# A hybrid DeltaNet and sliding-window trunk in fp32 on one core: decay chain, first chunk, norms by halves, and the order around the attention

## The chip, the cores and the metric

One core of one Trainium2 chip runs the whole program in one launch. The metric is device time in microseconds, from launch to the end of the last instruction, the median of three runs of the kernel before.

## What is computed

One sequence of 256 tokens of width 1024 goes through two layers, with an RMS norm ahead of each part:

```
h = x
h = h + gated_deltanet(norm(h))      # proj 1024 -> 4096 + 16, conv of 4 taps, silu, 8 heads of 128
h = h + swiglu(norm(h))              # dense, inner width 2816
k, v = norm(h) @ w_kv                # 4 kv heads of 64
h = h + attention(norm(h), k, v)     # 16 query heads, window 128, sinks, relative bias
h = h + moe(norm(h))                 # top 2 of 8 experts, inner width 3584
out = norm(h)

norm(x) = x * rsqrt(mean(x * x) + 1e-6) * w

# the delta rule, per head, over 4 chunks of 64 tokens, state S = 0 at first
v_new = u - w @ S
o     = q_dec @ S + attn @ v_new
S     = S * exp(g_last) + k_dec.T @ v_new
# g = cumsum(-exp(a_log) * softplus(a + dt_bias)), beta = sigmoid(b)
```

All inputs and the output are fp32.

## The kernel before

The program is written engine by engine: each of the five engines has its own block, a list of instructions in a fixed order, and semaphores (names `s_...`, `m_...`, `f_...`) tie them together. No scheduler sets an order; what a line waits for stands ahead of it as `wait_ge`. The tokens are two tiles of 128 (`NT`), a 1024-wide row of a tile is one row of SBUF. Products in the dense parts are made in three passes, high by high, low by high and high by low (`L1478` to `L1480` for TensorE); ScalarE rounds weights to their high part (`w_round`, L750), VectorE forms the rest (`w_rest`, L1144). The stages, in TensorE's order:

- **Projection and convolution.** 24 tiles of 128 columns of q, k and v come out of TensorE in six groups ("chunks" of weights) of four. Per tile ScalarE scales the first tap out of PSUM (`first_tap`, L663), VectorE adds the others (`convolve`, L974) and ScalarE applies silu (`conv_silu`, L649); at the first tile of a group `first_tap` also rounds a half of the next group's weights before and after the silu (`q_round`, L644). The decay chain (L676 to L681 on ScalarE: exponentials of the b columns, of `a_log` and of the a columns, then a logarithm, and a few small operations on VectorE between) stands behind the eighth tap. `squared` (L685) squares all of q, later all of k; `L1547` on TensorE sums the squares by matmuls with one column.
- **The delta rule.** TensorE computes u and w in four groups (L1631, L1641), ScalarE and VectorE evict them. Then the scan over four chunks (`n`): eight products w with S (L1654), eight q with S (L1660), VectorE's subtraction, eight products for the new state (L1667), eight with the masked scores (L1674). S is set to zero by a memset on GpSimd ahead of it.
- **Output projection.** Per tile, `turn_out` (L1682) transposes the output in two halves of four, ScalarE and VectorE evict one half each (`s_ot`), `project` (L1690) multiplies by two weight halves, and VectorE adds to h (`add_h`, L1135).
- **A norm** (`k` from 0 to 5: ahead of the DeltaNet, the dense SwiGLU, k and v, the attention, the router, and at the end) is a chain: ScalarE squares and sums a tile of 1024 columns (`squares`, L605), GpSimd makes the reciprocal root (`norm_rstd`, L510 and L511), VectorE multiplies by it and by the weights (`norm_x`, L933), TensorE transposes (`turn`, L1452), and ScalarE and VectorE evict to high and low parts (`turned`, L614 or L620, and L943 or L1155).
- **Dense SwiGLU**: eleven slices of the inner width, then keys and values.
- **Attention** in four groups of heads (`g`): VectorE and ScalarE prepare the queries (`queries`, L831), TensorE the scores, ScalarE the exponentials (`exps`, L841), TensorE transposes the weights and multiplies with v (`values`, L1849), VectorE divides (L1278), and `merge` (L1880) is the output product, by tiles of 128 columns of heads.
- **Router and experts**: 8 passes over 7 slices each, with weights of 2 MB that come by DMA, and then the last norm and the two transfers of the output at the end of the block of SyncE.

```
for n in range(8):                       # ScalarE, before
    first_tap(n)
act.wait_ge(s_tail, 1)
act.activation(beta, tail[:, :, 0:8], ACT.Exp, scale=-1.0).then_inc(s_bexp, 1)
```

## Time and profile before

| | |
|---|---|
| median of three runs | 1562.39 us (1561.8, 1562.39, 1566.46) |
| the profiled execution | 1561.36 us, of which the span 1559.5 |
| busy TensorE, its weight loads | 97%, 80% |
| busy VectorE, ScalarE, GpSimd | 72%, 58%, 7% |
| DMA | 438 MB, 281 GB/s on the mean |

Times of the trace are microseconds from the start of the span, and each number of the profile belongs to the one profiled execution. A row of a timeline is start, length, engine, line of the program, operation, output and inputs with their shapes, how many, and in square brackets how long the engine stood idle before it and what ended that. A row of waits is the waiting operation, what it waited for, and in microseconds the sum, how many, and the longest. A row of windows is given with its columns. The names in it are buffers: `ws` the large work space, `sm` the small one, `bank` the PSUM, `xn` the normed tokens, `cst` the constants.

### The profile page before, as it was taken

What the parts mean: (1) busy time and instruction counts of PE and PEld (TensorE: products, weight loads), DVE (VectorE), ACT (ScalarE), POOL (GpSimd) and SP (SyncE); (2) the same over time, 40 slices, a digit from 0 to 9 for tenths busy, and PEclk for the clock granted to TensorE, in tenths of its full rate; (3) what the DMA queues carried; (4) which work ended last, traced back from release to release, by engine and by line L of the source; (5) the groups of instructions that cost most, each with busy time, mean ns of one, the idle gap of its engine ahead of it and who ended that gap; (6) DMA issues with size and microseconds to landing.
All of it is one profiled execution on the core that took longest, in us unless ns stands there. A gap on an engine that the chain in (4) does not pass through costs nothing.

```text
span 1559.5 us, 22166 instructions
## 1 busy us (share of the span) xinstructions
PE 1505.5 (97%) x8759; PEld 1255.0 (80%) x8759; DVE 1126.2 (72%) x1048; ACT 903.2 (58%) x841; POOL 102.4 (7%) x63
## 2 busy tenths in 40 slices
PE   7999998999999889999999999999999999999996
PEld 6895976999987557888888888888888888888885
DVE  4656254555432348998998998889898889889885
ACT  4641133344422335776777777777777777677773
POOL 2331010000000000000000000000000000000000
PEclk9999999999999989999999999999999999999999
DMA  7432104655463156999999999999999999999992
GB/s 266 151 133 81 37 21 133 214 186 188 134 243 135 55 189 240 394 393 365 388 395 354 384 383 375 392 386 346 392 393 364 393 375 362 370 395 381 379 383 85
DMA packets 194028, 438.01 MB, mean 281 GB/s; under 512 B 5216, under 2 KB 28032, under 8 KB 193856
## 3 DMA queue, kind: packets, MB, share of 16 engines
q1 hardware_dynamic: 188944, 423.64, 73.9%
q0 software_dynamic: 2736, 9.31, 2.4%
q10 hardware_dynamic: 2304, 4.43, 0.8%
q8 instruction: 33, 0.54, 0.2%
q14 instruction: 11, 0.09, 0.0%
HBM read 429.48 MB, written 7.88 MB: 280 GB/s over the span
## 4 chain that ended last, share of the span: by engine, by line
PE 91%; DVE 4%; ACT 3%; issue 1%; DMA 1%; POOL 0%; DVEq 0%; ACTq 0%; POOLq 0%
PE bank L1478 24%; PE bank L1480 24%; PE bank L1479 24%; PE bank L1821 2%; PE bank L1690 2%; PE bank L1880 2%; PE bank L1513 2%; PE bank L1988 2%; PE bank L1866 1%; DVE ws L974 1%; DVE weights_lo L1144 1%; PE bank L1452 1%; PE bank L1620 1%; PE bank L1603 1%; PE bank L1547 1%
## 5 line engine op out<-in xcount | busy, mean ns | idle before, releaser
L1144 DVE TENSOR_TENSOR weights_lo<-weights,weights_hi 128x2048 fp32r<-128x2048 f32 (+1 forms) x396 | 823.5, 2122 | 152.3 <-ACT weights_hi L750 150.8
L750 ACT ACTIVATE weights_hi<-weights 128x2048 fp32r<-128x2048 f32 (+1 forms) x396 | 687.3, 1786 | 250.7 <-DMA weights<-in_moe_w_up 87.3
L1478 PE MATMUL bank<-weights_hi,expert_x_hi 128*128 128x512 f32 x896 | 354.9, 396 | 1.4 <-DVE expert_x_lo L1357 1.1
L1480 PE MATMUL bank<-weights_hi,expert_x_lo 128*128 128x512 f32 x896 | 349.4, 390 | 0.0
L1479 PE MATMUL bank<-weights_lo,expert_x_hi 128*128 128x512 f32 x896 | 349.2, 390 | 0.0
L1478 PE MATMUL bank<-weights_hi,hidden_hi 128*128 128x512 f32 x528 | 207.3, 393 | 2.1 <-DVE hidden_lo L1182 2.1
L1479 PE MATMUL bank<-weights_lo,hidden_hi 128*128 128x512 f32 x528 | 205.6, 389 | 0.0
L1480 PE MATMUL bank<-weights_hi,hidden_lo 128*128 128x512 f32 x528 | 205.6, 389 | 0.0
L1480 PEld LDWEIGHTS bank<-weights_hi,expert_x_lo 128*128 128x128 f32 x896 | 168.2, 188 | 36.4
L1478 PEld LDWEIGHTS bank<-weights_hi,expert_x_hi 128*128 128x128 f32 x896 | 168.3, 188 | 35.4 <-DVE expert_x_lo L1357 1.2
L1479 PEld LDWEIGHTS bank<-weights_lo,expert_x_hi 128*128 128x128 f32 x896 | 168.4, 188 | 33.4
L1478 PEld LDWEIGHTS bank<-weights_hi,hidden_hi 128*128 128x128 f32 x528 | 99.2, 188 | 22.5 <-issue 1.7
L1480 PEld LDWEIGHTS bank<-weights_hi,hidden_lo 128*128 128x128 f32 x528 | 99.1, 188 | 20.9
L1479 PEld LDWEIGHTS bank<-weights_lo,hidden_hi 128*128 128x128 f32 x528 | 99.2, 188 | 19.8
L1478 PE MATMUL bank<-x_hi,weights_hi 128*128 128x256 f32 x320 | 91.0, 284 | 1.2 <-issue 1.2
L1480 PE MATMUL bank<-x_hi,weights_lo 128*128 128x256 f32 x320 | 90.6, 283 | 0.0
L1479 PE MATMUL bank<-x_lo,weights_hi 128*128 128x256 f32 x320 | 90.5, 283 | 0.0
L767 ACT ACTIVATE ws<-bank 128x512 f32<-128x512 f32 x67 | 39.7, 593 | 84.9 <-PE bank L1480 84.7
L1478 PEld LDWEIGHTS bank<-x_hi,weights_hi 128*128 128x128 f32 x320 | 61.4, 192 | 1.8 <-issue 1.4
L1479 PEld LDWEIGHTS bank<-x_lo,weights_hi 128*128 128x128 f32 x320 | 61.4, 192 | 0.4
L1480 PEld LDWEIGHTS bank<-x_hi,weights_lo 128*128 128x128 f32 x320 | 61.4, 192 | 0.0
L1478 PE MATMUL bank<-qkv_x_hi,qkv_hi 128*128 128x256 f32 x192 | 57.5, 300 | 3.2 <-DVE ws L974 3.2
(306 smaller groups left out, 1553.3 us busy)
## 6 DMA issues: line engine op xcount, KB each, us to landing
weights<-in_moe_w_down SPq DMA_DIRECT2D x56, 2048.0 KB, 9.5
weights<-in_moe_w_up SPq DMA_DIRECT2D x56, 2048.0 KB, 9.5
weights<-in_moe_w_gate SPq DMA_DIRECT2D x55, 2048.0 KB
weights<-in_a_w_in SPq DMA_DIRECT2D x8, 2048.0 KB, 9.0
weights<-in_ffn_w_up SPq DMA_DIRECT2D x11, 1024.0 KB, 5.3
weights<-in_ffn_w_gate SPq DMA_DIRECT2D x11, 1024.0 KB, 7.9
weights<-in_ffn_w_down SPq DMA_DIRECT2D x11, 1024.0 KB, 4.9
weights<-in_a_w_out SPq DMA_DIRECT2D x2, 2048.0 KB, 7.9
```

What stands on the lines that cost most here:

```text
L750: act.activation(hi[:, j * n:(j + 1) * n], slot[k][:, j * n:(j + 1) * n], ACT.Copy).then_inc(w_hi[k], 1)
L767: act.activation(act_h, bank[0][:, :], ACT.Silu).then_inc(m.act, 1)
L974: i_ = dve.scalar_tensor_tensor(out=dst[:, sh:T], in0=src[:, 0:T - sh], scalar=cw[:, w:w + 1], in1=dst[:, sh:T], op0=ALU.mult, op1=ALU.add)
L1144: dve.tensor_tensor(to[:, c], slot[k][:, c], hi[:, c].bitcast(F32), ALU.subtract).then_inc(w_lo[k], 1)
L1478: pe.matmul(dst, ah, bh, start=start, stop=False, skip_group_check=True)
L1479: pe.matmul(dst, ah, bl, start=False, stop=False, skip_group_check=True)
L1480: return pe.matmul(dst, al, bh, start=False, stop=stop, skip_group_check=True)
L1513: m = pe.matmul(b[:, :], xt[:, kt, t * P:(t + 1) * P], g8[c % 3][:, kt, :], start=kt == 0, stop=kt == KT - 1)
L1690: m = pe.matmul(bank[banks[q]][:, :], xt[:, kt, t * P:(t + 1) * P], g8[slots[q]][:, kt, :], start=kt == 0, stop=kt == KT - 1)
L1821: m = pe.matmul(bank[3 + g % 2][:, j * T:(j + 1) * T], g8[k][:, kt, c], xt[:, kt, :], start=kt == 0, stop=kt == KT - 1)
L1880: m = pe.matmul(bank[2 * t + q][:, :], oT[:, kt, t * P:(t + 1) * P], g8[q][:, kt, :], start=first and kt == kts[0], stop=last and kt == kt ...
L1988: m = pe.transpose(bank[2][:, j * P:(j + 1) * P], hid[:, j * P:(j + 1) * P], ident)
```

## The change

It has five parts, all in the order or the form of instructions:

- **Decay chain.** ScalarE's four small activations go ahead of the first tap, VectorE's operations between them ahead of its first tile. The rounding of the second group's weights moves with them, out of the first `first_tap`.
- **First chunk.** With S = 0, the new values are u, the new state is `k_dec.T @ u` and the output `attn @ u`. The eight products of w and of q with S, the subtraction and the scaled evictions of the first chunk are gone, the loops run over chunks 1 to 3, and the two sets of products that stay (`chunk_tail(0, u)`) stand between the first and the last two groups of u and w. VectorE copies state and output out of PSUM (four copies). GpSimd's memset is gone.
- **Norms by halves.** Squares, multiplications and their semaphores count halves of 512 columns. GpSimd adds the two partial sums and the 1e-6 in one operation. `turn` waits per half, the last transfers go by halves.
- **Output projection.** It waits per half of the transposed output. The first tile's transposes for the next norm stand between the two halves of the second tile's product, the small bucket product (L1704, now L1791) behind the first tile of the up projection. VectorE adds and norms the first tile before the rests of the first up weights. The second slice's gate weights go into the free half of buffer 0.
- **Attention.** `exps(g + 1)` stands ahead of `queries(3)`, and `merge` goes in more pieces: four tiles of the first half before the wait for the third group's heads, two tiles of the second token tile before the wait for the fourth's.

Cut to its core, in the order of the file (small memories, GpSimd, ScalarE, VectorE, TensorE):

```diff
-        ss = view(sm, 0, 6, NT)
+        ss = view(sm, 352, 5, NT, 2)
...
-                    pool.wait_ge(s_ss, 2 * k + t + 1)
-                    rstd(rs[:, k, t:t + 1], ss[:, k, t:t + 1], half2[:, 0:1], s_rstd, 1.0 / D)
+                    pool.wait_ge(s_ss, 4 * r + (t + 3 if k == 5 else 2 * t + 2))
+                    a = rs[:, r, t:t + 1]
+                    link(pool.tensor_scalar(a, ss[:, r, t, 0:1], ss[:, r, t, 1:2], EPS, ALU.add, ALU.add))
+                    pool.tensor_tensor(a, a, half2[:, 0:1], ALU.pow).then_inc(s_rstd, 1)
...
-            pool.memset(S, 0.0).then_inc(s_S, 1)
...
+            def square(k, t, q, h_done=None, count=0):
+
+                if h_done is not None:
+                    act.wait_ge(h_done, count)
+                act.activation(sq_junk[:, 2 * t + q, :], h[:, t, q * 512:(q + 1) * 512], ACT.Square, scale=D ** -0.5,
+                               accum_out=ss[:, rstd_of(k), t, q:q + 1]).then_inc(s_ss, 1)
+
             def squares(k, h_done=None, base=0, tiles=range(NT)):
-                k = rstd_of(k)
                 for t in tiles:
-                    if h_done is not None:
-                        act.wait_ge(h_done, base + 2 * t + 2)
-                    act.activation(xt_junk, h[:, t, :], ACT.Square, accum_out=ss[:, k, t:t + 1]).then_inc(s_ss, 1)
-                    if t == 0:
-                        act.wait_ge(s_ss, 2 * k + 1)
+                    for q in range(2):
+                        square(k, t, q, h_done, base + 2 * t + q + 1)
...
-                ahead = n % 4 == 0 and c < 6
+                ahead = n and n % 4 == 0 and c < 6
...
-            act.wait_ge(s_cw, 1)
-            for n in range(8):
-                first_tap(n)
-
             act.wait_ge(s_tail, 1)
             tail = view(bank[5], 0, NT, 16)
             act.activation(beta, tail[:, :, 0:8], ACT.Exp, scale=-1.0).then_inc(s_bexp, 1)
             act.wait_ge(s_small, 16 * 4)
             act.activation(alog, alog, ACT.Exp).then_inc(s_soft, 1)
+            for j in range(2):
+                q_round(1, j)
             act.wait_ge(s_nx, 1)
             link(act.activation(nx, nx, ACT.Exp))
             act.activation(nx, nx, ACT.Ln, bias=K("one")).then_inc(s_soft, 1)
+            act.wait_ge(s_cw, 1)
+            for n in range(8):
+                first_tap(n)
...
-            for n in range(NC):
+            for n in range(1, NC):
                 t, par = divmod(n, 2)
                 r = slice(par * C, par * C + C)
-                act.wait_ge(s_omm, 2 * n + 1)
-                if n == 0:
+                act.wait_ge(s_omm, 2 * n)
+                if n == 1:
                     act.wait_ge(s_egq, 1)
-                if n:
-                    act.wait_ge(s_o, n)
+                act.wait_ge(s_o, n)
...
+            squares(1, s_h, 0, [0])
             w_round(ffn, 1, 0)
+            turned(1, (0, 1))
             act.wait_ge(s_first_f, 16)
             for j in range(2):
                 act.activation(view(whi[0], 1024 * j, 4, FS), first_gate[:, 4 * j:4 * j + 4, :],
                                ACT.Copy).then_inc(w_hi[0], 1)
-            squares(1, s_h, 0)
-            turned(1)
+            squares(1, s_h, 0, [1])
+            turned(1, (2, 3))
...
-            w_round(ffn, 0, 1, f_g, 1)
+            w_round(ffn, 0, 1, to=whi[0][:, 2048:4096])
...
+                if g < 3:
+                    exps(g + 1)
                 if g == 0:
                     queries(3)
-                if g < 3:
-                    exps(g + 1)
...
-            act.wait_ge(m_h, 4)
-            squares(5)
+            for q in range(2):
+                for t in range(NT):
+                    square(5, t, q, m_h, 2 * q + t + 1)
...
-                dve.scalar_tensor_tensor(out=xn[:, t, :], in0=h[:, t, :], scalar=rs[:, r, t:t + 1],
-                                         in1=rows[k % 2][:, :], op0=ALU.mult, op1=ALU.mult).then_inc(s_xn, 1)
+                for q in range(2):
+                    c = slice(q * 512, (q + 1) * 512)
+                    dve.scalar_tensor_tensor(out=xn[:, t, c], in0=h[:, t, c], scalar=rs[:, r, t:t + 1],
+                                             in1=rows[k % 2][:, c], op0=ALU.mult, op1=ALU.mult).then_inc(s_xn, 1)
...
-            for ct in range(8):
-                convolve(ct)
...
-            for ct in range(8, 10):
+            for ct in range(10):
...
-            for g in range(4):
+            def applied(g):
                 dve.wait_ge(s_umm, g + 1)
                 dve.tensor_copy(u[:, 4 * g:4 * g + 4, :], bank[g % 2][:, :].rearrange("p (a b) -> p a b", b=DH)).then_inc(s_u, 1)
+
+            applied(0)
+            applied(1)
+            r = slice(0, C)
+            dve.wait_ge(s_smm, 1)
+            for q in range(2):
+                i_ = dve.tensor_copy(S[:, 4 * q:4 * q + 4, :], bank[[5, 7][q]][:, :].rearrange("p (a b) -> p a b", b=DH))
+            i_.then_inc(s_S, 1)
+            dve.wait_ge(s_omm, 1)
+            for q in range(2):
+                i_ = dve.tensor_copy(o[r, 4 * q:4 * q + 4, :], bank[[4, 6][q]][r, :].rearrange("p (a b) -> p a b", b=DH))
+            i_.then_inc(s_o, 1)
+            applied(2)
+            applied(3)
...
+            add_h(0, s_wo_mm, 0, (2, 3, 4, 0), 0)
+            norm_x(1, 0)
             w_rest(ffn, 1, 0)
+            x_rest(0)
             for j in range(2):
                 dve.wait_ge(w_hi[0], j + 1)
                 dve.tensor_tensor(view(wlo[0], 1024 * j, 4, FS), first_gate[:, 4 * j:4 * j + 4, :],
                                   view(whi[0], 1024 * j, 4, FS).bitcast(F32), ALU.subtract).then_inc(w_lo[0], 1)
-            add_h(0, s_wo_mm, 0, (2, 3, 4, 0), 0)
-            norm_x(1, 0)
             add_h(1, s_wo_mm, 0, (2, 3, 4, 0), 0)
-            x_rest(0)
...
-                    pe.wait_ge(s_xn, 2 * k + t + 1)
                     for q in range(2):
+                        pe.wait_ge(s_xn, 4 * k + 2 * t + q + 1)
...
+            def chunk_tail(n, new):
+
+                t, par = divmod(n, 2)
+                r = slice(par * C, par * C + C)
+                if n < NC - 1:
+                    for hh in range(H):
+                        m = pe.matmul(bank[[5, 7][hh // 4]][:, (hh % 4) * DH:(hh % 4 + 1) * DH], kd[r, t * H + hh, :],
+                                      new[r, hh, :], start=True, stop=True)
+                    m.then_inc(s_smm, 1)
+                if n:
+                    pe.wait_ge(s_o, n)
+                for hh in range(H):
+                    m = pe.matmul(bank[[4, 6][hh // 4]][r, (hh % 4) * DH:(hh % 4 + 1) * DH], aT[r, t * H + hh, :],
+                                  new[r, hh, :], start=True, stop=True)
+                m.then_inc(s_omm, 1)
+
             for g in range(4):
+                if g == 2:
+                    pe.wait_ge(s_u, 2)
+                    chunk_tail(0, u)
...
+                        if kt % 4 == 0:
+                            pe.wait_ge(s_ot, 2 * t + kt // 4 + 1)
...
-            pe.wait_ge(s_ot, 2)
-            pe.wait_ge(s_o1, NC)
+            pe.wait_ge(s_o1, NC - 1)
             project(0, (2, 0), (3, 4), (2, 3), s_wo_mm)
             turn_out(1)
-            pe.wait_ge(s_ot, 4)
-            project(1, (2, 0), (3, 4), (4, 0), s_wo_mm)
+            project(1, (2, 0), (3, 4), (4, 0), s_wo_mm, [0])
             turn(1, [0])
-
-            pe.wait_ge(s_relb, 16)
-            pe.matmul(bank[2][0:QH, 0:RELS + 1], relb[0:BUCKETS, :], K("bucket_hot")[0:BUCKETS, :],
-                      start=True, stop=True).then_inc(s_brow, 1)
+            project(1, (2, 0), (3, 4), (4, 0), s_wo_mm, [1])
...
+            merge(0, range(4))
             pe.wait_ge(s_oT2, 3)
-            merge(0, range(6))
+            merge(0, range(4, 6))
             values(3)
+            merge(1, range(2), [0])
             pe.wait_ge(s_oT2, 4)
             merge(0, range(6, 8))
-            merge(1, range(8), [0])
+            merge(1, range(2, 8), [0])
```

ScalarE around the decay chain. `sm` are the small columns (beta, decays), `qkv_hi` the rounded weights, L663 is the first tap and L649 the silu. Before, behind the eighth tap:

```order
L676 ACTIVATE sm<-bank 128x16
L678 ACTIVATE sm<-sm 128x8
L680 ACTIVATE sm<-sm 128x16
L681 ACT_TABLE_LOAD
L681 ACTIVATE sm<-sm,cst 128x16
L644 ACTIVATE qkv_hi_62<-weights_49 128x2048
L649 ACT_TABLE_LOAD
L649 ACTIVATE ws<-ws 128x256
L644 ACTIVATE qkv_hi_62<-weights_49 128x2048
L663 ACTIVATE ws<-bank,sm 128x256
```

Of the change, ahead of the first tap of all:

```order
L678 ACTIVATE sm<-bank 128x16
L680 ACTIVATE sm<-sm 128x8
L650 ACTIVATE qkv_hi_62<-weights_50 128x2048 x2
L684 ACTIVATE sm<-sm 128x16
L685 ACT_TABLE_LOAD
L685 ACTIVATE sm<-sm,cst 128x16
L669 ACTIVATE ws<-bank,sm 128x256
L655 ACT_TABLE_LOAD
L655 ACTIVATE ws<-ws 128x256
```

The four activations moved ahead of the first tap (L669), with the second group's rounding (L650, twice) between them.

TensorE at the start of the scan. L1631 and L1641 are u and w of one group; 64x128 and 128x128 are the outputs. Before:

```order
L1631 MATMUL bank<-ws 64x128 x16
L1641 MATMUL bank<-ws 128x64 x16
L1654 MATMUL bank<-ws 64x128 x8
L1660 MATMUL bank<-ws 64x128 x8
L1667 MATMUL bank<-ws 128x128 x8
L1674 MATMUL bank<-ws 64x128 x8
```

Of the change, where L1652 and L1658 are the products for the state and with the masked scores:

```order
L1672 MATMUL bank<-ws 64x128 x16
L1682 MATMUL bank<-ws 128x64 x16
L1652 MATMUL bank<-ws 128x128 x8
L1658 MATMUL bank<-ws 64x128 x8
L1672 MATMUL bank<-ws 64x128 x16
L1682 MATMUL bank<-ws 128x64 x16
L1695 MATMUL bank<-ws 64x128 x8
```

The first chunk's two remaining products moved ahead of the last pairs of u and w, and the first L1695 is now that of the second chunk.

TensorE at the second tile of the output projection: L1682 then L1711 are the transposes of the output, L1690 then L1721 its product, L1452 then L1474 the transposes of the next norm. Before:

```order
L1682 MATMUL bank<-cst,ws 128x128 x8
L1690 MATMUL bank<-weights_51,xt 128x512 x8
L1690 MATMUL bank<-weights_49,xt 128x512 x8
L1452 MATMUL bank<-cst,xn 128x128 x8
L1704 MATMUL bank<-cst,sm 16x256
```

Of the change:

```order
L1711 MATMUL bank<-cst,ws 128x128 x8
L1721 MATMUL bank<-weights_51,xt 128x512 x8
L1474 MATMUL bank<-cst,xn 128x128 x8
L1721 MATMUL bank<-weights_49,xt 128x512 x8
L1500 MATMUL bank<-weights_hi_56,x_hi 128x256
```

The transposes of the first tile's norm moved from behind the product to between its halves; the bucket product (L1704) no longer stands ahead of the up projection.

## Rows read from the trace of the kernel before

**Rows 1.** The page, busy time, share of the span and instructions of each engine.
```profile
PE 1505.5 (97%) x8759; PEld 1255.0 (80%) x8759; DVE 1126.2 (72%) x1048; ACT 903.2 (58%) x841; POOL 102.4 (7%) x63
```

**Rows 2.** Waits of TensorE: who <- for whom: us in all, times, longest.
```profile
PE bank L1478 <- DVE ws L974: 3.2, 1, 3.2
PE bank L1849 <- DVE ws L1274: 2.7, 1, 2.7
...
PE bank L1478 <- DVE x_lo L1155: 2.0, 1, 2.0
PE bank L1880 <- DVE ws L1278: 1.8, 2, 1.0
PE bank L1690 <- ACT xt L737: 1.5, 2, 0.7
```

**Rows 3.** Windows: length, busy PE, PEld, DVE, ACT, POOL, PEclk, DMA share, GB/s.
```profile
62.00:66.00 4.00, 4.00 (x20) 3.91 (x20) 3.33 (x8) 1.24 (x4) 2.26 (x1) 0.50 0.90 340
66.00:70.00 4.00, 4.00 (x29) 4.00 (x29) 2.77 (x6) 2.56 (x4) 0.00 (x0) 0.78 0.02 4
192.00:196.00 4.00, 4.00 (x28) 3.84 (x26) 1.28 (x2) 0.00 (x0) 0.00 (x0) 0.74 1.09 365
516.00:520.00 4.00, 3.78 (x32) 2.57 (x32) 3.92 (x22) 1.84 (x5) 0.00 (x0) 0.79 0.53 216
520.00:524.00 4.00, 4.00 (x35) 3.06 (x36) 0.17 (x1) 3.44 (x18) 0.00 (x0) 0.50 0.03 6
```

**Rows 4.** ScalarE's timeline around the fifth and the ninth first tap.
```profile
38.66 0.46 ACT L663 ACTIVATE ws<-bank,sm 128x256 f32<-128x256 f32 x1
...
42.94 0.45 ACT L663 ACTIVATE ws<-bank,sm 128x256 f32<-128x256 f32 x1
...
50.51 1.28 ACT L676 ACT_TABLE_LOAD   x1
...
59.53 0.45 ACT L663 ACTIVATE ws<-bank,sm 128x256 f32<-128x256 f32 x1
```

**Rows 5.** The chain that ended last, at the column sums: start, length, engine, line.
```profile
89.96 8.66 PE bank L1547 x64
```

**Rows 6.** ScalarE's timeline, its second square.
```profile
87.73 1.91 ACT L685 ACTIVATE ws<-ws 128x2048 f32<-128x2048 f32 x1
```

**Rows 7.** TensorE's timeline over the scan's first chunk.
```profile
190.80 3.53 PE L1654 MATMUL bank<-ws 128*64 128x128 f32 x16 [1.23 <-issue]
...
196.01 2.05 PE L1667 MATMUL bank<-ws 64*128 64x128 f32 x16
...
200.31 0.87 PE L1654 MATMUL bank<-ws 128*64 128x128 f32 x6 [0.36 <-DVE ws L1110]
```

**Rows 8.** VectorE's timeline at the norm behind the dense SwiGLU.
```profile
448.83 1.29 DVE L933 SCALAR_TENSOR_TENSOR xn<-h,sm,norm_row 128x1024 f32<-128x1024 f32 x1 [2.25 <-POOL sm L511]
...
451.38 0.69 DVE L943 COPY xt<-bank 128x512 f32<-128x512 f32 x1
```

**Rows 9.** ScalarE's timeline at the same norm.
```profile
446.62 1.06 ACT L605 ACTIVATE ws<-h 128x1024 f32<-128x1024 f32 x1 [8.09 <-DVE h L1135]
```

**Rows 10.** ScalarE's timeline ahead of the experts.
```profile
576.68 3.71 ACT L750 ACTIVATE weights_hi<-weights 128x2048 fp32r<-128x2048 f32 x2 [2.79 <-DMA weights<-in_moe_w_up]
```

**Rows 11.** The chain that ended last, at the exponentials of group 1.
```profile
511.89 3.19 ACT ws L841 x16
```

**Rows 12.** ScalarE's timeline behind the last add.
```profile
1550.97 1.06 ACT L605 ACTIVATE ws<-h 128x1024 f32<-128x1024 f32 x1 [5.07 <-DVE h L1368]
```

**Rows 13.** VectorE's timeline, the last norm's two tiles.
```profile
1553.19 1.28 DVE L933 SCALAR_TENSOR_TENSOR xn<-h,sm,norm_row 128x1024 f32<-128x1024 f32 x1 [2.26 <-POOL sm L511]
1555.20 1.29 DVE L933 SCALAR_TENSOR_TENSOR xn<-h,sm,norm_row 128x1024 f32<-128x1024 f32 x1 [0.72 <-POOL sm L511]
```

**Rows 14.** GpSimd's timeline, its step for the last norm's second tile.
```profile
1553.39 1.14 POOL L510 TENSOR_SCALAR sm<-sm 128x1 f32<-128x1 f32 x1 [0.33 <-ACT ws L605]
```

**Rows 15.** DMA issues of the last 10 us: KB each, us to landing.
```profile
out<-xn SPq DMA_DIRECT2D x2, 512.0 KB, 2.6
```

66 lines of the change are left out of this document (30 added, 36 removed).

## The prediction

> **What bounds the kernel now.** The page first: TensorE is busy 97% of the span [rows 1], and its expert loop from 620 us on shows no wait worth naming. So only what TensorE waits for, and what its clock loses behind a wait, can be taken away. The waits of TensorE [rows 2]: the reader is to see five entries, all short, all in the stages around the two dense loops. Then the windows of the stretches behind three of them [rows 3]: there the granted clock is 0.50 to 0.79, the lower of the two levels (1.2 against 2.4 GHz) for part of the window, though the engine is busy for 4.00 of 4.00 us (3.78 in one). A wait can thus cost nearly twice its length. After that, for each part of the change, the timeline of the engine that is waited for.
>
> The sum is made against the profiled execution, 1561.36 us (span 1559.5 and 1.9 around it); the median of the runs, 1562.39, lies 1.0 above it.
>
> **Decay chain.** At its ninth convolution tile ScalarE runs the decay chain: behind the eighth tap comes a table load at 50.51, and the next tap only at 59.53, 9.0 us later [rows 4]. One chunk earlier the same place, with the rounding of a new chunk but without the chain, takes from the end of the tap at 38.66 (0.46 long) to the next at 42.94, 3.8 us. Moved ahead of the first tap, the chain lies in ScalarE's idle time there (its instructions are table loads of 1.28 and four others of 0.2 to 0.3), which hides it; if that cover were gone, every tap would be up to 2 us later, and the taps have about that much slack. So the taps from the ninth on come 5.2 us earlier. TensorE waited 3.2 us there [rows 2], and its clock was 0.50 and 0.78 of full in the next two windows [rows 3], worth 2.0 and 0.9 us. With the taps 5.2 us earlier the third chunk's matmuls end before the wait's condition is late: gain 3.2 + 2.9 = 6.1. What is late next: the column sums of squares on TensorE begin at 89.96 [rows 5] and need ScalarE's second square, 87.73 to 89.64 [rows 6]. That moves up by 5.2 and TensorE by 6.1, so 0.8 is given back. Term: **-5.3** (ends -3.2, if the clock falls all the same, and -6.1).
>
> **Zero state.** The scan's first chunk costs, from the last multiplication of u and w to the second chunk's start at 200.31: a wait of 1.2 for the last eviction of w, then 190.80 to 200.31, 9.5 us, 3.5 of it for eight products where the following eights take 2.0 each [rows 7], at a granted clock of 0.74 [rows 3]. Of this the state products (196.01) and those with the mask (behind them, to 199.95), 3.9 together, stay, and move between the two pairs of u and w; the products with w and q, the subtraction, the eight scaled evictions and the added output go. The new copies (state 2, output 2) have no row; each is bounded by nothing and by the 0.69 of a 128x512 copy [rows 8], which I take; they lie under TensorE's second pair of u and w. The wait of 1.2 stays, now before the second chunk. Gain: 10.7 - 3.9 - 1.2 = 5.6 if the clock stays up, 4.0 if it falls behind the same wait as before, costing the same 1.6. A like wait has just shown the lower level, so I take **-4.0** (ends -3.0 and -5.6). The memset on GpSimd that goes was hidden.
>
> **Projection.** TensorE waits 1.5 in two times for both evictions of the turned output [rows 2]; the first matmuls need one of the two. The half that is waited for no longer is 0.5 each: **-1.0** (0 to -1.5).
>
> **Norm in the projection's middle.** The first tile's add, squares and norm now run under the second tile's projection, and the wait of 2.0 for x_lo [rows 2] goes, for its cover is half of the second tile's projection. The second tile's chain (add 0.7, half a square, GpSimd, half a norm) then ends some 0.3 us after its cover, the first up-projection tile and the bucket product. The rounding of the gate into the other half of its buffer changes nothing: ScalarE takes it up behind a silu that waits for the same matmuls. **-1.8** (-1 to -2.3).
>
> **Norms by halves elsewhere.** A square of 1024 columns takes 1.06 [rows 9] and VectorE's norm 1.29 [rows 8], so TensorE can begin about 0.9 earlier. But at the norm behind the dense loop VectorE does two adds, 1.3 together, between its norm, which ends at 450.12, and the eviction at 451.38 that the next matmuls need [rows 8], and those keep their place: **-0.3** (0 to -0.9). Ahead of the router the longest path is another: ScalarE rounds the first expert's up weights at 576.68, as they land [rows 10], and only then computes the exponential that the gates wait for. The transfer waits for the end of the attention output, not for the norm. **0** (to -1.1, if the transfer were not last). At the start GpSimd's second power and VectorE's norms leave **-0.1** (0 to -0.6).
>
> **Attention.** ScalarE copies the last queries and only then, at 511.89, exponentiates group 1, 3.2 us [rows 11]; TensorE waits 2.7 for the weights [rows 2] and has a clock of 0.79 and 0.50 in the two windows behind [rows 3], worth 0.8 and 2.0. With exponentials ahead of queries both go. The two waits for the copied heads, 1.8 in all [rows 2], are now covered by four and by one further tile of the output product. Late next is group 2: its exponentials still stand behind the evictions of group 1, and with 3.2 for them and about 1 until the first weights are ready, against TensorE's scores of group 3, its margin comes out near zero. **-7.3** (ends -3 and -8).
>
> **End.** From the last add to the end of the last norm it is 1550.97 to 1556.49, 5.5 us, and the first tile's norm ends at 1554.47, 3.5 behind the add [rows 12, 13]. The last half needs such a single chain, with half a square (0.4 less), since the squares of the first tile and of the first halves are already done: 3.1. To this comes GpSimd's turn: its last step was stretched to 1.14 beside a norm [rows 13, 14], where it needs nothing like that alone; I assume that it now waits out the first tile's norm, 1.1, so 4.2 and a gain of 1.3. The last transfer is half as large: between nothing and 1.3, half of its 2.6 [rows 15]; I take 0.7. **-2.0** (-1.0 to -3.0).
>
> The Trainium skill (SBUF — State Buffer, the section on the two separate sides) says that VectorE and GpSimd share a port pair which one of them holds for a whole instruction. By that rule GpSimd would be let in between the two halves, after 0.6 instead of 1.1, and the result would be 0.5 lower; the stretched step [rows 14] agrees with the lock, but with one instruction beside it, it cannot tell the two apart.
>
> Sum: 5.3 + 4.0 + 1.0 + 1.8 + 0.3 + 0.1 + 7.3 + 2.0 = 21.8. The profiled execution would be 1539.6, the median **1540.6 us**.
>
> **The rivals.**
> - *A wait takes the place of the one removed, in the attention.* Group 2's exponentials come too late by 1 to 2 us, and the clock falls again behind that wait. For it: the margin near zero. Against it: the steps after it have 10 us of output product as cover. The term halves, 3.7 are lost: 1544.3.
> - *The clock stays up* behind the wait that is left ahead of the second chunk, and recovers sooner by the router. 1.6 and about 1 more: 1538.0. For it: the waits for the copied heads [rows 2] are not followed by a window like these; against it the first row of [rows 7].
> - *The halves do not do what they say*: each wait for a norm is in truth one for the step beside it, as at the router. Then 1.8, 0.3 and 2.0 fall away: 1544.7.
> - *Slower than before*: the code ahead of the three loops gets another length, and with it the loop bodies another place; if each pass paid more for its jump or its instruction fetch, nothing would hide it, since TensorE is the bound. There are 11 dense slices and 56 expert slices; from 0.32 us each (21.8 / 67) the whole gain is eaten, and at 0.5 us the result is 1574.1. Against it: the same engines execute the same bodies, and TensorE shows no wait at a pass's start.
>
> **How the numbers follow.** The forecast, to within some 3 us, has 0.50; the attention rival 0.20; the clock 0.16; the halves 0.10; the loop rival 0.02; and 0.02 that most of the waits only move. 0.3% of this kernel, 4.7 us, is about what a measurement can tell from no change. The first four cases are all beyond it: faster 0.96, same 0.02, slower 0.02. With every term at its short end the sum is 11 us and the time 1551; at its long end 28 and 1534; that all fall on one side is less than 2 in 10, so the range is 1535 to 1548.5.
>
> **What would show it.** In the profile after: no entry of 3.2 at the fourth chunk and a granted clock of 1.00 from 58 to 70 us; a wait of 0.5 to 1 at the sums of squares; about 5 us of state and mask products between the two pairs of u and w, and a wait near 1.2 ahead of the second chunk; waits of 0.2 instead of 0.7 at the projection; the first up-projection tile directly behind the projection; no 2.7 at the second group of values; still the same 8.5 us from the end of the output product to the landing of the up weights. The prediction is wrong if a wait of more than 1.5 us stands in the attention, if the clock is low in a stretch where it was full before, or if a pass of the expert loop has changed by more than 0.05 us.

## The result, and the profile after

The changed kernel takes **1542.86 us** in the median (five runs, 1540.88 to 1545.77) against 1562.39 for the kernel before (1559.78 to 1566.46): ratio 0.9869, 95% interval 0.9856 to 0.9883, so 18 to 22 us less. 1540.6 was forecast, in a range of 1535 to 1548.5. The execution that was traced took 1545.63, 2.8 above that median, and every number from a trace below is its own.

First the page of the changed kernel: busy time by engine, to be held against [rows 1].

```profile
PE 1501.1 (97%) x8727; PEld 1249.7 (81%) x8727; DVE 1125.6 (73%) x1052; ACT 898.2 (58%) x851; POOL 98.9 (6%) x62
```

And, from the same page, the chain that ended last, its shares of the span by engine.

```profile
PE 76%; DMA 9%; DVE 6%; ACT 5%; issue 3%; POOL 0%; DVEq 0%; SPq 0%; ACTq 0%
```

TensorE's busy time fell by only 4.4 us, the span by 15.7: mostly waits are gone. The chain holds a surprise, to which we come back: in the kernel before, TensorE had 91% of it and DMA 1%.

The waits of TensorE, beside [rows 2]: who waits for whom, us in all, times, longest.

```profile
PE bank L1474 <- DVE xn L944: 11.9, 2, 10.1
PE bank L1500 <- DVE hidden_lo L1204: 3.1, 4, 1.5
...
PE bank L1500 <- DVE expert_x_lo L1379: 1.6, 2, 1.1
...
PE bank L1695 <- issue: 1.2, 1, 1.2
...
PE bank L1569 <- ACT ws L692: 1.1, 1, 1.1
...
PE bank L1721 <- ACT xt L743: 0.7, 2, 0.3
```

Of the five entries of rows 2, four are gone (3.2, 2.7, 2.0, 1.8) and the fifth is halved (L1690, now L1721: 1.5 to 0.7). New is the 1.1 ahead of the column sums (L1569) that the prediction named. The waits for `hidden_lo` and `expert_x_lo` in the expert loop are new only in part. The kernel before has these two entries, which rows 2 leaves out:

```profile
PE bank L1478 <- DVE hidden_lo L1182: 2.1, 2, 1.5
...
PE bank L1478 <- DVE expert_x_lo L1357: 1.1, 1, 1.1
```

So three waits came in, two for `hidden_lo` (0.37 and 0.65) and one for `expert_x_lo` (0.52), 1.5 us together; the prediction did not name them.

The windows of the same columns as [rows 3]: the fourth group's tiles, the column sums, the scan's start, the first query product (L1850, before L1821).

```profile
62.00:66.00 4.00, 4.00 (x36) 4.00 (x35) 3.19 (x4) 4.00 (x5) 0.00 (x0) 1.00 0.71 271
86.00:90.00 4.00, 4.00 (x24) 4.00 (x24) 2.20 (x6) 1.56 (x4) 0.31 (x1) 0.60 0.98 374
90.00:94.00 4.00, 4.00 (x20) 4.00 (x21) 0.73 (x2) 0.42 (x1) 0.00 (x0) 0.50 0.03 11
...
192.00:196.00 4.00, 3.79 (x35) 3.54 (x34) 1.30 (x2) 0.53 (x3) 0.00 (x0) 1.00 1.02 333
...
464.00:468.00 4.00, 4.00 (x16) 3.36 (x16) 0.00 (x0) 0.00 (x0) 0.00 (x0) 0.79 0.80 314
```

The clock is 1.00 where the wait of 3.2 stood and at the scan's start, and 0.50 to 0.60 in the column sums. In the first query product it is 0.79, where the kernel before has 1.00 (its window from 476 to 480).

TensorE's timeline at the sums and over the scan's start, beside [rows 5] and [rows 7].

```profile
83.89 11.16 PE L1569 MATMUL bank<-cst,ws 128*128 128x1 f32 x64 [1.05 <-ACT ws L692]
...
182.96 2.00 PE L1652 MATMUL bank<-ws 64*128 64x128 f32 x16
...
191.75 1.93 PE L1695 MATMUL bank<-ws 128*64 128x128 f32 x16 [1.23 <-issue]
...
199.94 1.31 PE L1695 MATMUL bank<-ws 128*64 128x128 f32 x10 [0.36 <-DVE ws L1132]
```

The state and mask products stand ahead of the last u and w, and the wait of 1.2 is now ahead of the second chunk. Each of these products is two instructions in the trace: x16 is eight products, and the x64 of the sums is 32 products of one column.

The end, beside [rows 13 to 15]: first VectorE's timeline, the last norm.

```profile
1538.56 2.75 DVE L944 SCALAR_TENSOR_TENSOR xn<-h,sm,norm_row 128x512 f32<-128x512 f32 x4 [1.10 <-POOL sm L523]
```

GpSimd's timeline, its two steps for the second tile.

```profile
1538.52 0.30 POOL L522 TENSOR_SCALAR sm<-sm 128x1 f32<-128x1 f32 x1
1538.90 0.84 POOL L523 TENSOR_TENSOR sm<-sm,cst 128x1 f32<-128x1 f32 x1
```

The DMA issues of the last 10 us: KB each, us to landing.

```profile
out<-xn SPq DMA_DIRECT2D x4, 256.0 KB, 2.0
```

One norm of four halves without a gap takes the place of two tiles with 0.72 between. GpSimd's last step ends at 1539.74, beside the second of the four halves and before the third, the first that needs it.

### The profile page after: what moved, and what is told of

It reads as the page before. It is cut to its first block, busy times and chain, and to the rows that moved or that the text cites. A ratio compares the mean times of both kernels' runs of the same rounds, so it can differ in the third digit from the quotient of the medians.

```text
span 1543.8 us, 22118 instructions
## 1 busy us (share of the span) xinstructions
PE 1501.1 (97%) x8727; PEld 1249.7 (81%) x8727; DVE 1125.6 (73%) x1052; ACT 898.2 (58%) x851; POOL 98.9 (6%) x62
## 4 chain that ended last, share of the span: by engine, by line
PE 76%; DMA 9%; DVE 6%; ACT 5%; issue 3%; POOL 0%; DVEq 0%; SPq 0%; ACTq 0%
PE bank L1500 19%; PE bank L1502 19%; PE bank L1501 19%; DMA weights<-in_moe_w_gate 6%; DVE weights_lo L1166 3%; PE bank L1850 2%; PE bank L1721 2%; PE bank L1909 2%; PE bank L1535 2%; ACT weights_hi L756 2%; DMA weights<-in_moe_w_down 2%; PE bank L2020 1%; DVE ws L985 1%; DMA weights<-in_moe_w_up 1%; ACT qkv_hi L650 1%
## 5 line engine op out<-in xcount | busy, mean ns | idle before, releaser
L1502 PEld LDWEIGHTS bank<-weights_hi,hidden_lo 128*128 128x128 f32 x528 | 99.1, 188 | 20.9
L1501 PEld LDWEIGHTS bank<-weights_lo,hidden_hi 128*128 128x128 f32 x528 | 99.2, 188 | 19.7
L1200 DVE TENSOR_TENSOR ws<-ws,bank 128x512 f32<-128x512 f32 x67 | 45.7, 682 | 18.5 <-issue 14.5
```

Of the source, the lines that this page charges most:

```text
L1200: dve.tensor_tensor(hid, act_h, bank[1][:, :], ALU.mult).then_inc(m.hid, 1)
L1501: pe.matmul(dst, ah, bl, start=False, stop=False, skip_group_check=True)
L1502: return pe.matmul(dst, al, bh, start=False, stop=stop, skip_group_check=True)
```

## The experiments

One execution is a poor witness for a few microseconds, so the first run repeats the changed kernel, and a later one the kernel before. Times are medians; kernels of one paragraph whose times are compared ran on the same chip (the scan's first chunk below is compared by ratio, across two chips). A ratio with its interval comes from all runs and need not be that of the two medians.

**The changed kernel again.** No edit.

> The changed kernel a second time. Theory 1 (the three waits of TensorE inside the expert loop, 0.37, 0.52 and 0.65, and the low clock behind the last query and key norm, worth 1.7, are scatter of one execution): the median is again 1541 to 1545, but the waits in the loop stand at other places or are fewer, and the first scores product takes 14.0 instead of 15.7. Theory 2 (they belong to the new order): the same waits at the same places, and 15.7 again.

1544.51 us, where the kernel before had 1564.22 on that chip (ratio 0.9874, interval 0.9856 to 0.9892). The low clock behind the last norm ahead of the attention was not there: the first query product (the expectation calls it the first scores product) took 14.05 here, 15.74 in the first trace. Extra waits in the loop were there again, 0.20 in the first pass and a long one in the last, here in TensorE's timeline:

```profile
1466.36 0.49 PE L1500 MATMUL bank<-weights_hi,hidden_hi 128*128 128x512 f32 x1 [1.78 <-DVE hidden_lo L1204]
```

So neither theory holds whole: the loop's waits come back, the low clock does not. Whether that clock is mere scatter stays open: of all fourteen traces here, the product took 15.74 in five of the ten with the new norms and 14.05 in the other five and in all four with the old ones.

**The kernel before again.** No edit.

> The kernel before a second time, for its trace. If the small waits inside the expert loop of the changed kernel (0.2 to 1.8, near its second and last pass) are scatter of the weights' transfers, this trace has one or more of them too, at 630 to 720 or 1470 to 1490 us. If they belong to the new order, the loop is again without a wait, as in the first trace. The column products at the start take 4.9 or 6.9: both were seen in the kernels with the change, so both may be here.

1565.45 us. Beside the waits that the loop has in both orders (1.1, 0.3 and 0.6 in the first pass, 1.5 at the end) it has one of 0.18, in the last pass. Its column sums were unlike those of its first trace (8.82 without a wait, 89.80 to 98.62), here in its second trace, TensorE's timeline:

```profile
87.40 12.82 PE L1547 MATMUL bank<-cst,ws 128*128 128x1 f32 x64 [1.23 <-ACT ws L685]
```

So a wait ahead of the sums and slow sums belong to both kernels, in some executions. With two traces of each kernel the stages can be told apart from scatter. Each stage is the distance between two marks on TensorE; in the last column is what the prediction's terms give for it.

| stage (TensorE) | before, two traces | changed, two traces | mean change | forecast |
|---|---|---|---|---|
| start to the first u | 181.85, 184.38 | 179.23, 177.88 | -4.6 | -5.4 |
| to the output projection | 42.12, 40.52 | 36.04, 37.42 | -4.6 | -4.5 |
| to its second tile | 15.62, 15.61 | 15.19, 15.19 | -0.4 | -0.5 |
| to the second gate slice | 31.20, 32.72 | 29.44, 29.44 | -2.5 | -1.8 |
| dense loop to the first query product | 202.38, 202.37 | 202.19, 202.19 | -0.2 | -0.3 |
| attention and output product | 94.92, 96.07 | 89.31, 87.62 | -7.0 | -7.3 |
| router to the first expert | 21.75, 22.07 | 22.52, 22.55 | +0.6 | 0 |
| experts to the last scatter | 956.32, 956.84 | 958.75, 960.45 | +3.0 | 0 |
| to the end | 13.34, 13.32 | 11.13, 11.16 | -2.2 | -2.0 |

**The decay chain, undone** (with the rounding of the second group and VectorE's operations, which go back to their old places as well).

```diff
+            act.wait_ge(s_cw, 1)
+            for n in range(8):
+                first_tap(n)
+
             act.wait_ge(s_tail, 1)
...
-            act.wait_ge(s_cw, 1)
-            for n in range(8):
-                first_tap(n)
```

> The changed kernel with the decay chain back behind the eighth tap. As I read the two traces, the move is worth 6.1 up to the column sums and gives 3.3 plus a wait of 1.05 back there: so this one should be 2 to 2.6 slower than the changed kernel, near 1545.2, with the wait of 3.2 at the fourth group and the sums at 8.8. Rival (the prediction's own figure): 5.3 slower, near 1548.2.

1549.46 us, 4.95 above the changed kernel on the same chip (ratios to before 0.9902, interval 0.9886 to 0.9918, against 0.9874). The wait is back with its size: 3.48 at the fourth group. The expectation, read off a single pair of traces, was 2 to 2.6; by the median the prediction's 5.3 was nearer, by the traces it was not. In its own trace the sums took 9.33 without a wait where the repeated changed kernel had 11.45 with 1.24 of wait, and up to the marks behind them this trace is 2.9 later than the repeat and 1.6 later than the first of the changed kernel. By the ratios the part is worth 4.4, with nearly 4 either way. So it is worth something between 1.6 and 5, and these runs do not say where.

**The second square earlier.** Could the wait ahead of the sums be had for free?

```diff
                 if n:
                     conv_silu(n - 1)
+                if n == 16:
+                    squared(n)
                 if ahead:
                     q_round(c, 1)
```

> The second square moves ahead of a rounding on ScalarE, so TensorE should not wait 1.05 ahead of the column sums. Theory 1 (that wait brings the fall of the clock forward): wait gone, the sums take 8.8 as in the kernel before instead of 11.2, and the tiles behind them 12.4 instead of 13.3; with the wait 4.3 less, near 1538.6. Rival (the narrow sums pull the clock down by themselves, however they are reached): only the wait goes, 1.0 less, near 1541.9.

1541.86 us, 2.65 under the repeated changed kernel (ratio 0.9855, interval 0.984 to 0.9871). That is the rival's time; the sums are theory 1's. The wait is gone and the sums take 9.29; the tiles behind them, 13.49, did not get shorter. TensorE's timeline:

```profile
82.97 9.29 PE L1569 MATMUL bank<-cst,ws 128*128 128x1 f32 x64
```

So a wait goes with an earlier fall of the clock: in the nine traces with the sums in one piece they took 10.7 to 12.8 behind a wait (five) and 8.8 to 9.3 without one (four). But the clock comes down without one too: in the kernel before, with no idle time since 61.59, it fell inside the sums, which run from 89.80 to 98.62. Its windows, columns as in [rows 3]:

```profile
90.00:94.00 4.00, 4.00 (x38) 4.00 (x37) 2.67 (x6) 1.08 (x3) 2.16 (x1) 1.00 0.72 227
94.00:98.00 4.00, 4.00 (x25) 4.00 (x26) 1.67 (x4) 1.20 (x3) 0.00 (x0) 0.64 0.78 302
98.00:102.00 4.00, 4.00 (x20) 4.00 (x21) 0.26 (x2) 0.00 (x0) 3.01 (x1) 0.51 0.00 0
```

38 instructions in 4 us at 1.00, then 25 at 0.64, with TensorE busy for all of it. Only 0.6 us of the third window are still sums. What one of their instructions costs at the low clock is read in the changed kernel's window from 90 to 94 above, which lies inside its sums: 20 at 0.50, so 0.2 against 0.105 for one.

**The sums in two halves.** If one long stretch of them lowers the clock, two short ones may not. `sums(0)` is the half for the first square, `sums(1)` that for the second, each behind its own wait.

```diff
+            sums(0)
             qkv(4)
-            pe.wait_ge(s_sq, 2)
-            for a_ in range(2):
-                for un in range(NU):
...
-            m.then_inc(s_sumsq, 1)
+            sums(1).then_inc(s_sumsq, 1)
```

> Half of the column sums stands ahead of the fifth group's tiles, the other half behind. Theory 1 (one long stretch of narrow products lowers the clock, two short ones do not): all 64 take 6.7 together (0.105 each) instead of 11.2, the wait of 1.05 is gone, the tiles behind take 12.0: 6 to 7 less, near 1536.5. Rival (any such stretch lowers it): the clock falls twice, the sums take 8.8 or more, and the gain is at most the wait, 1541.9, or there is none.

1536.61 us, 7.9 under the repeated changed kernel: ratio to before 0.9828 (0.9811 to 0.9846). TensorE's timeline:

```profile
69.68 3.63 PE L1568 MATMUL bank<-cst,ws 128*128 128x1 f32 x32
...
84.57 3.63 PE L1568 MATMUL bank<-cst,ws 128*128 128x1 f32 x32
```

7.3 for both, no wait (the second half reaches TensorE 3.6 later, when the square is done), and the next wait mark, at 108.86 in the repeated changed kernel, stands at 102.35. The clock still fell, but behind the second half and for less time. The windows of this kernel:

```profile
84.00:88.00 4.00, 4.00 (x39) 4.00 (x38) 2.20 (x6) 1.56 (x4) 0.95 (x1) 1.00 0.50 145
88.00:92.00 4.00, 4.00 (x24) 4.00 (x24) 1.38 (x5) 0.42 (x1) 2.47 (x1) 0.59 0.97 373
```

And over the whole stretch, first the repeated changed kernel, then this one:

```profile
82.00:102.00 20.00, 19.48 (x115) 19.48 (x116) 6.17 (x15) 3.58 (x9) 8.38 (x2) 0.66 0.30 106
82.00:102.00 20.00, 19.98 (x160) 19.78 (x158) 12.26 (x24) 5.15 (x13) 13.11 (x5) 0.91 0.32 107
```

A mean clock of 0.91 instead of 0.66 over 20 us is worth 5.0, and the wait of 1.24 is gone: 6.2 of the 6.5 by which this trace reaches the first u earlier (171.37 against 177.88). So "leaves the clock up" is too strong: the two short stretches themselves ran at full clock, and the low stretch behind them is shorter than the one that began inside the long one. This is the best single edit of the study. Run once more as the base of the last four kernels it gave 1537.08 (0.9826, interval 0.9813 to 0.984), with 3.63 twice.

> The split sums a second time, as the base for the three kernels beside it: ratio 0.983 again. Theory (two short stretches of narrow products leave the clock up): all 64 sums take 7.3 and the tiles behind them start within 0.2 us of the last. If the first trace was luck, the sums take 9 or more here.

**The scan's first chunk, undone.** The eights of products with a zero state, the subtraction, the scaled evictions and the memset are back.

```diff
-                if g == 2:
-                    pe.wait_ge(s_u, 2)
-                    chunk_tail(0, u)
...
-            for n in range(1, NC):
+            for n in range(NC):
```

> The changed kernel with the scan's first chunk as it was (all eights of products, the subtraction, the scaled evictions, the memset). The two traces give 5.7 for this part, since the clock stays up through the state and mask products: so 5.7 slower than the changed kernel, near 1549.5, with a granted clock under 0.8 behind the last eviction of w and 3.5 for the first eight products. Rival (the prediction's own 4.0, the clock falls in both): 4.0 slower, near 1547.8, and no low clock that the changed kernel lacks.

1546.68 us, ratio 0.988 (0.986 to 0.9899). Against the changed kernel's 0.9874 that is 1 us, with some 4 of uncertainty: the time does not decide. The traces do, on TensorE's own marks. TensorE's timeline of this kernel, whose clock is 0.74 in the window from 188 to 192:

```profile
186.96 3.45 PE L1683 MATMUL bank<-ws 128*64 128x128 f32 x16 [1.23 <-issue]
...
196.39 1.96 PE L1683 MATMUL bank<-ws 128*64 128x128 f32 x16 [0.36 <-DVE ws L1123]
```

From the first u to the third chunk it takes 26.3 (178.01 to 204.32); the changed kernel took 20.7 with 1.93 for its first eight products, and 22.1 in its second trace, where they took 3.12 at a clock of 0.87 and 0.70, here in its timeline:

```profile
190.41 3.12 PE L1695 MATMUL bank<-ws 128*64 128x128 f32 x16 [1.23 <-issue]
```

Against this trace, in which the clock fell, the part is worth 5.6 when the changed kernel's clock stays up and 4.2 when it falls: the prediction's 5.6 and 4.0, and an execution picks one. But the old order has both too: 3.53 in the first trace of the kernel before, 1.93 in its second, where the same stretch takes 24.8 (184.38 to 209.18) and the part is worth 4.1 or 2.7.

**The attention alone**, put into the kernel before, whole and then only its exchange of two calls, the first hunk here.

```diff
-                if g == 0:
-                    queries(3)
                 if g < 3:
                     exps(g + 1)
+                if g == 0:
+                    queries(3)
...
+            pe.wait_ge(s_oT2, 2)
+            merge(0, range(4))
             pe.wait_ge(s_oT2, 3)
-            merge(0, range(6))
+            merge(0, range(4, 6))
             values(3)
+            merge(1, range(2), [0])
```

> The kernel before with the attention's new order alone (exponentials ahead of the last queries, output product in more pieces). Theory 1: 7.3 less than before, ratio 0.9953: the wait of 2.7 and both waits for copied heads (1.8) go, and the granted clock is 1.00 from 510 to 535 us. Rival (the exponentials of group 2 come too late and a wait takes the old one's place): 3.7 less, ratio 0.9976, with a wait of 1 to 2 ahead of the weights of group 2.

> The kernel before with only the two calls on ScalarE exchanged. Theory 1: of the 7.3, the wait of 2.7 and its 2.8 of lost clock, so 5.5 less than before, ratio 0.9965; the two waits of 1.0 and 0.8 for copied heads stay as they are. Rival (the pieces of the output product are what counts): under 2 less.

1555.17 and 1559.14 us against 1564.46: ratios 0.9948 (0.9931 to 0.9964) and 0.9958 (0.9941 to 0.9974), so 8.1 and 6.6 less, with 2.6 either way (the medians alone say 9.3 and 5.3). The stage on TensorE, from the first query product to the router, takes 87.95 and 89.50 in their traces, against 94.92 and 96.07 in the two of the kernel before: 7.0 to 8.1 and 5.4 to 6.6 less. A window behind the place where the wait of 2.7 stood, of the whole order:

```profile
520.00:524.00 4.00, 4.00 (x42) 2.96 (x44) 2.85 (x19) 2.53 (x10) 0.00 (x0) 1.00 0.00 0
```

The same window of the exchange alone:

```profile
520.00:524.00 4.00, 4.00 (x59) 3.35 (x60) 0.85 (x2) 3.74 (x18) 0.00 (x0) 1.00 0.59 238
```

And the exchange alone, waits of TensorE:

```profile
PE bank L1880 <- DVE ws L1278: 1.8, 2, 1.0
```

The clock stays at 1.00 in both, no wait takes the old one's place, and the pieces of the output product are what removes the last line, 1.8. The rivals fall.

**The router.** Two edits on top of the split sums: wide products into a free bank in TensorE's waits (the expectation says five, the kernel has six, the last one, of 256 columns, outside this cut), and VectorE's slot positions ahead of the gate weights.

```diff
+                    filler(2, 384)
                     turn(4, [1])
+                    filler(1, 384)
...
             m.then_inc(s_log, 1)
+            filler(2)
```

```diff
-            dve.wait_ge(s_ge, 1)
-            link(dve.tensor_scalar(den2[:, :, 0], gt[:, :, 1], 1.0, None, ALU.add))
...
             dve.wait_ge(s_posmm, 1)
...
+            dve.wait_ge(s_ge, 1)
+            link(dve.tensor_scalar(den2[:, :, 0], gt[:, :, 1], 1.0, None, ALU.add))
```

> The split sums, and five wide products of constants into a free bank in TensorE's waits around the router (they compute nothing that is read). Theory 1 (the low clock there comes from the waits among narrow products): granted clock 1.00 from the router to the experts, the second half of the router product 1.9 instead of 3.6, the first gather 3.3 instead of 6.3; VectorE, busy behind it, lets about 1.9 us through: near 1.9 less than the split sums alone. Rival (the narrow products lower it by themselves, or the fillers come too late): the clock stays at 0.50 and the kernel is up to 1 us slower.

> The split sums, with VectorE's slot positions ahead of the gate weights, so that they do not wait for ScalarE's exponential. Theory 1 (by the timeline the exponential holds VectorE for 0.45, and the positions are then bound by TensorE's product at the low clock): the gather begins at most 0.4 earlier, no difference that can be measured. Rival (the exponential behind the rounding is what bounds the router): 1 to 2 less, and the wait of 0.7 ahead of the gather gone.

> Fillers and positions together. Theory 1: with the clock up the exponential is what VectorE would wait for, and this order takes it out of the way: 1.9 of the fillers and about 1.2 more, 3.1 less than the split sums, and 10 to 11 less than the changed kernel. Rival (VectorE's work behind the gather binds alone): no more than the fillers alone.

1537.51, 1539.86 and 1536.38 us beside the base's 1537.08; ratios 0.9832, 0.9838 and 0.9832, intervals of 0.003 to 0.004: no difference that a median can tell. The traces tell more. From the first router product to the first expert product it is 22.4 and 22.7 in the two traces of the base, 22.9 with fillers, 21.9 with positions first, and 19.7 with both. With the fillers alone the clock was still up in the second half of the router product, which took 1.92 instead of 3.55, as expected. All of it was lost in one longer wait ahead of the gather, behind which the clock fell after all: the gather took 6.16, not the 3.3 of the expectation. ScalarE's timeline of that kernel:

```profile
554.82 3.71 ACT L756 ACTIVATE weights_hi<-weights 128x2048 fp32r<-128x2048 f32 x2 [4.40 <-DMA weights<-in_moe_w_up]
558.43 0.19 ACT L884 ACTIVATE sm<-sm 128x2 f32<-128x2 f32 x1
```

VectorE's timeline:

```profile
558.65 0.17 DVE L1336 TENSOR_SCALAR sm<-sm 128x2 f32<-128x2 f32 x1 [3.35 <-ACT sm L884]
```

The waits of TensorE:

```profile
PE bank L1976 <- DVE ws L1348: 3.9, 1, 3.9
```

The exponential stands behind the rounding of weights that have just landed, as the prediction read it from [rows 10]; whoever makes the rest faster waits for it. In this stage the fillers alone are worth nothing, the positions alone 0.6, both together 2.8, each read from a single trace; of the 3.1 expected for both, the median shows 0.7 and the ratio nothing. The expectation of 1.9 for the fillers alone was wrong because it took VectorE's own work for the only limit.

## Why the prediction was right, and where it was not

The median is 2.3 above the forecast. The table above rests on two traces of each kernel. The other ten share most of its stages with one of the two, and over all that share a stage the changes are: start -4.5 (four old, three new), scan -4.1 (four, nine), the projection's middle -2.9 (four, ten), attention -7.0 (two, ten), router +0.2 (four, seven), expert loop +1.7 (four, ten). The rest is as in the table. These figures sum to -19.4; the medians differ by 19.5.

**Decay chain: -5.3 forecast.** Mechanism right: no wait and a clock of 1.00 from 58 to 66 us, and a wait of 1.05 at the sums where 0.5 to 1 was forecast. The stage with the start gives -4.5, the undo 1.6 to 5. What the step left out is that the sums behind it run at either clock and between 8.8 and 12.8 us in both kernels, so that a wait of 1 there can cost 2 more.

**Zero state: -4.0.** Against an old trace whose clock fell in the first eight products it is 4.2 or 5.6 by execution. The step took that fall in the kernel before for given; three of the four traces of the old order do not have it, and against the second trace of the kernel before the part is 2.7 or 4.1. The stage with the halved waits for the turned output gives -4.1 against -4.5, so the forecast's size holds on the mean, partly by luck.

**Projection and the norm in its middle: -1.0 and -1.8.** The waits went from 0.74 to 0.34 each, and the up-projection follows the projection directly; the stage is 1.76 shorter against the first trace of before, as forecast, and 3.3 against the second, which ran there at a clock of 0.65 for a while. The first trace is the exception: the other three of the old order take 32.7 for the stage. So the term was read off the one execution without that loss, and is nearer to 2.9.

**Norms by halves: -0.3 and 0.** -0.2 behind the dense loop. At the router the wait for the norm fell from 2.6 to 1.75, and yet nothing was won: the up weights are rounded 8.5 us after the end of the output product in both kernels (568.25 to 576.68, 551.56 to 560.07), and the gather begins 14.5 behind it in both. It then runs 6.4 instead of 5.7, at the low clock. That is the +0.6 of the table, and it is within the scatter: the stage takes 21.8 to 23.9 in the four old traces and 22.4 to 22.9 in seven new ones.

**Attention: -7.3.** -7.0 by the stages, -8.1 by the ratio of the kernel with this part alone. The margin near zero held.

**End: -2.0.** -2.2, of which 0.5 is the shorter tail behind the last norm: from its end to the span's end 3.0 before, 2.5 now. I had assumed that GpSimd's step waits until both halves of the norm are through, 1.1 on the path. It did not: it began at 1538.90, took 0.84 and was over at 1539.74, while the four halves ran from 1538.56 to 1541.31 without a gap. It was not on the path at all: the third half, the first that needs it, starts at 1539.91, right behind the second. So the norm ends 3.85 behind the last add (1537.46), not 4.2. The Trainium skill (SBUF — State Buffer, the section on the two separate sides) has the port pair held for one instruction at a time; by that rule GpSimd could get in between two halves. The 0.84 instead of the 0.57 that the same step took just before at 1537.85 is in line with that, but the second half is no longer than the others, so the trace does not show the hand-over itself.

**What the sum did not have: the expert loop.** It is +3.0 in the table and +1.7 over all traces: 956.3 to 956.8 in four of the old order, 956.9 to 960.5 in ten of the new. This is the step that came out otherwise. The prediction gave the stage no term, since the trace before shows no wait worth naming there, and never asked what keeps the loop's weights in time. Without the loop the stages sum to 20.9 less in the table and to 21.1 over all traces, of 21.8 forecast; the loop makes up most of the 2.3 by which the forecast was missed. Of the three signs that the prediction gave for being wrong, one stayed away (no wait over 1.5 in the attention) and two came: the low clock in the first query product in the first trace, and passes of the loop that changed by more than 0.05 us.

A pass without a wait is as long as ever (119.12 us, 1041.29 to 1160.41), so the rival of a dearer jump or fetch falls. The loss stands at waits in the first, the second and the last pass. In the first trace these are the 0.37, 0.52 and 0.65. In the repeat they are 0.20 and 1.78, and behind the 1.78 the clock fell, so that the slice with it took 20.48 instead of 16.82 us. The windows of the repeat there:

```profile
1464.00:1468.00 4.00, 2.22 (x9) 1.53 (x8) 3.92 (x3) 3.65 (x2) 0.00 (x0) 0.94 1.05 390
1468.00:1472.00 4.00, 4.00 (x13) 3.13 (x12) 3.38 (x3) 1.58 (x2) 0.00 (x0) 0.63 1.01 399
```

The chain that ended last leads from such waits to transfers. Start, length, work, in the changed kernel:

```profile
603.52 9.23 DMA weights<-in_moe_w_gate
...
636.18 11.27 DMA weights<-in_moe_w_gate
...
1429.56 12.99 DMA weights<-in_moe_w_down
```

The same 2 MB take 9.2 or 11 to 13 us, and behind the slower ones a rest of VectorE came late and TensorE with it, here in its timeline:

```profile
649.34 0.49 PE L1500 MATMUL bank<-weights_hi,hidden_hi 128*128 128x512 f32 x1 [0.37 <-DVE hidden_lo L1204]
```

But a slow transfer alone does not make a wait. The kernel before has such transfers too, and TensorE waits nowhere in its loop between 613.65 and 1539.46. One of them, from its DMA issues between 722 and 723:

```profile
weights<-in_moe_w_up SPq DMA_DIRECT2D x1, 2048.0 KB, 13.9
```

Nor is the chain's share of DMA a clean measure, for the chain leaves TensorE only where TensorE waited. DMA has 1% of it in the kernel before's first trace (and none of it expert weights of the loop), 3% in the one of its second, 9% here and 6% in the repeat; but in the kernel with the positions first DMA has 1%, and the loop still waits once for 0.95.

From the wait at the first hidden product to the last scatter the five traces in which that product came after 602 us took 932.5 to 933.1, the nine in which it came before 600 took 933.8 to 936.7. One of the five is the kernel with the scan's first chunk undone (602.04), which has the new order everywhere else, so that order by itself does not bring the loss. That the earlier start is the cause is not shown: it may be what else the transfers meet at that time, and no run here held the stages and moved the loads. The cause stays open.

## What to carry to other kernels

A wait of TensorE among narrow or small products cost its own length here and, in some executions, about as much again or more in clock, so removing it can pay twice. A long stretch of one-column products was worth cutting in two with wide products between, although the clock still fell behind it. Price each removed wait together with what is late next, and look for that also in the stage that shows almost no wait: the expert loop here gave 1.7 us of the gain back. And before a single pair of traces decides between figures a few microseconds apart, take a second trace of each kernel, and use every other kernel's trace that shares the stage.

## What was not expected of the hardware

- The granted clock fell to the lower level inside a stretch in which TensorE was busy without a gap (4.00 of 4.00 us, no wait since 61.59), in 32 one-column products of two instructions each: 38 instructions per 4 us, then 25, and 20 where the whole window is at 0.50. The same products in two stretches of 16, with 11.3 to 12.8 us of 256-column products between, ran at full clock in four of five traces (3.63 each); in the fifth the second took 4.87. But in all five the clock fell for some us close by: behind the first stretch in three (0.57 to 0.66 on the mean of 4 or 5 us), behind or in the second in four (0.59 from 88 to 92 in the first of these traces).
- The same kernel takes different clock paths: the sums 8.82 or 12.82, the scan's first eight products 3.53 or 1.93, the first query product 14.05 or 15.74. The runs of one kernel on one chip spread over 2 to 8 us.
- One-column sums behind a wait of 1.0 to 1.3 us took 10.7 to 12.8 us in five traces, without a wait 8.8 to 9.3 in four.
